# A two-slot ring of weight sums in block 0: ScalarE in place of the load queue issues the stores

## What is computed

```python
h = x + W_out( sig(g_pool) * PoolBranch(n) + sig(g_attn) * W_attn_up(SWA(n)) )    # n = RMSNorm(x)
h = h + W_down( relu(RMSNorm(h) @ W_up)**2 )
y = RMSNorm_final(h)
```

## Time and profile before

| | |
|---|---|
| median of 3 runs | 2518.96 us (2517.32 to 2522.46) |
| the profiled execution | 2517.32 us, span 2515.7 us |
| PE busy | 2372.8 us, 94% of the span |
| DVE, ACT, POOL busy | 1594.0, 1091.8, 345.9 us |
| mean granted TensorE clock | 0.981 of full speed |

### The profile page before, as it was taken

The page is one execution under the profiler, slowest core; times in us unless marked ns, Lnnn a source line. Parts: engine busy times, 40 slices in busy tenths (PEclk is TensorE's granted clock), DMA queues, the critical chain, the costliest instruction groups (busy, mean ns, idle before and its releaser), DMA issues.

```text
span 2515.7 us, 41191 instructions
## 1 busy us (share of the span) xinstructions
PE 2372.8 (94%) x16389; PEld 2192.5 (87%) x16389; DVE 1594.0 (63%) x2432; ACT 1091.8 (43%) x1922; POOL 345.9 (14%) x296
## 2 busy tenths in 40 slices
PE   8999988888788999999999999899999999899997
PEld 8999987878787787999998787899998777799997
DVE  7655733333357556867777656777868655678766
ACT  4533423131343434554553534555554433545543
POOL 1400333333333400000002400000002400000000
PEclk9999999999999999999999999999999999999998
DMA  4223444444455233676674223676665223566774
GB/s 159 73 83 98 151 159 159 160 162 156 166 177 198 66 98 119 230 231 203 203 260 163 73 87 109 218 226 201 219 219 208 95 82 95 190 199 198 231 227 170
DMA packets 149165, 410.37 MB, mean 163 GB/s; under 512 B 17520, under 2 KB 17872, under 8 KB 144880
## 3 DMA queue, kind: packets, MB, share of 16 engines
q1 hardware_dynamic: 144240, 399.00, 48.5%
q10 hardware_dynamic: 4736, 8.75, 0.9%
HBM read 349.65 MB, written 58.13 MB: 162 GB/s over the span
## 4 chain that ended last, share of the span: by engine, by line
PE 66%; DMA 11%; DVE 8%; POOL 6%; ACT 3%; issue 3%; SPq 1%; DVEq 0%; POOLq 0%; ACTq 0%
PE prod L528 30%; DMA weight_split<-wsplit 7%; PE auxB L747 6%; PE auxB L749 6%; PE auxB L748 6%; PE prod L747 5%; PE prod L749 5%; PE prod L748 5%; DMA weight_sums<-wsum 4%; POOL wsum L1644 2%; POOL wsum L1645 2%; POOL wsum L1646 2%; POOL wsum L1643 2%; DVE wring L1183 1%; PE auxB L528 1%
## 5 line engine op out<-in xcount | busy, mean ns | idle before, releaser
L528 PE MATMUL prod<-nH,wm 128*128 128x272 f32 (+1 forms) x3104 | 732.5, 337 | 49.0 <-DVE wm L1183 35.5
L528 PEld LDWEIGHTS prod<-nH,wm 128*128 128x128 f32 x3104 | 507.9, 192 | 112.5 <-issue 39.2
L792 ACT ACTIVATE wm<-raw 128x1024 fp32r<-128x1024 f32 x232 | 234.9, 1012 | 627.0 <-PE prod L528 477.2
L1183 DVE TENSOR_TENSOR wm<-raw,wm 128x1024 fp32r<-128x1024 f32 x232 | 288.1, 1242 | 255.1 <-ACT wm L792 254.1
L528 PE MATMUL prod<-nL,wm 128*128 128x272 f32 (+1 forms) x1552 | 443.4, 335 | 0.0
L792 ACT ACTIVATE wring<-rawq 128x512 fp32r<-128x512 f32 x492 | 307.2, 629 | 285.4 <-PE auxB L749 173.5
L1183 DVE TENSOR_TENSOR wring<-rawq,wring 128x512 fp32r<-128x512 f32 x492 | 334.9, 686 | 102.8 <-PE auxB L749 80.0
L528 PE MATMUL prod<-midH,wm 128*128 128x272 f32 (+1 forms) x1664 | 349.0, 321 | 41.4 <-DVE wm L1183 28.9
L528 PEld LDWEIGHTS prod<-midH,wm 128*128 128x128 f32 x1664 | 263.0, 195 | 64.0 <-issue 24.4
L528 PEld LDWEIGHTS prod<-nL,wm 128*128 128x128 f32 x1552 | 268.0, 192 | 26.7 <-issue 0.5
L747 PE MATMUL auxB<-n7H,wring 128*128 128x256 f32 x768 | 220.5, 287 | 24.6 <-ACT zt L792 14.1
(11 more groups left out here) (173 smaller groups left out, 4477.7 us busy)
## 6 DMA issues: line engine op xcount, KB each, us to landing
raw<-weights SPq DMA_DIRECT2D x200, 512.0 KB, 3.6
wring<-weight_split SPq DMA_DIRECT2D x180, 512.0 KB, 4.1
rawq<-weights SPq DMA_DIRECT2D x288, 256.0 KB, 4.2
rawq<-weight_sums SPq DMA_DIRECT2D x204, 256.0 KB, 4.1
weight_split<-wsplit SPq DMA_DIRECT2D x20, 1536.0 KB, 9.5
weight_sums<-wsum SPq DMA_DIRECT2D x12, 1024.0 KB, 8.0
raw<-weights SPq DMA_DIRECT2D x32, 320.0 KB, 2.8
y<-hT ACTq DMA_DIRECT2D x12, 512.0 KB, 2.8
```

What stands on the lines that cost most here:

```text
L528: ins = nc.tensor.matmul(out[:, s, 0:hi - lo], lhs, rhs[:, lo:hi], start=first, stop=last)
L792: return nc.scalar.activation(out, in_, ACT.Copy, scale=scale)
L1183: return tt(out, x, f(high), ALU.subtract)
```

## The change

ScalarE takes over all stores of the sums. At the end of each odd unit n of block 0's MLP it issues the 1.5 MB store of pair n // 2 (`sums_out`, in split phases, after `s_SL`), then waits for the sums of the **next** pair n // 2 + 1, makes their high part and issues their first store (`sums_high`; in the phases 1, 3, 5 this is the only store, the 1 MB one). Pair 0 is handled before the first unit. DVE's `sums_low` moves from the odd unit of its pair to the even one. SP has no store left between its loads, and its waits for `s_S` and `s_SL` on behalf of the stores go.

```diff
@@ SP
-            def store_sums(p):
-                s, ph = p % 2, p // PAIRS
-                if ph in SPLIT_PHASES:
-                    at = SPLIT_PHASES.index(ph) * PAIRS + p % PAIRS
-                    wait(sp, s_S, p)
-                    sp.dma_start(sums_d[p, :, 3, :], wsum[s][:, 3, :]).then_inc(set_out[s], 16)
-                    wait(sp, s_SL, p)
-                    sp.dma_start(split_d[at], f(wsplit[s][:, :, :, :])).then_inc(set_out[s], 16)
-                else:
-                    wait(sp, s_S, p)
-                    sp.dma_start(sums_d[p], wsum[s][:, :, :]).then_inc(set_out[s], 16)
...
-                if n % 2 and n >= 7:
-                    store_sums((n - 7) // 2)
...
-                    if b == 1 and i in (1, 3, 5):
-                        store_sums(PHASES * PAIRS - 3 + i // 2)
@@ ACT
-            def sums_high(n):
-                p = n // 2
-                if n % 2 == 0 and p // PAIRS in SPLIT_PHASES:
-                    wait(act, s_S, p)
-                    copy(wsplit[p % 2][:, :, 0, :], wsum[p % 2][:, 0:3, :]).then_inc(s_SH.sem, 1)
+            def sums_high(p):
+
+                st, split = p % 2, p // PAIRS in SPLIT_PHASES
+                wait(act, s_S, p)
+                if split:
+                    copy(wsplit[st][:, :, 0, :], wsum[st][:, 0:3, :]).then_inc(s_SH.sem, 1)
+                    act.dma_start(sums_d[p, :, 3, :], wsum[st][:, 3, :]).then_inc(set_out[st], 16)
+                else:
+                    act.dma_start(sums_d[p], wsum[st][:, :, :]).then_inc(set_out[st], 16)
+
+            def sums_out(p):
+                ph = p // PAIRS
+                if ph in SPLIT_PHASES:
+                    wait(act, s_SL, p)
+                    at = SPLIT_PHASES.index(ph) * PAIRS + p % PAIRS
+                    act.dma_start(split_d[at], f(wsplit[p % 2][:, :, :, :])).then_inc(set_out[p % 2], 16)
+
+            def sums_step(n):
+                if n % 2:
+                    sums_out(n // 2)
+                    if n // 2 + 1 < PHASES * PAIRS:
+                        sums_high(n // 2 + 1)
...
-                    sums_high(n)
+                    sums_step(n)
...
                 if b == 0:
                     root("h", 0)
+                    sums_high(0)
@@ DVE
             def sums_low(n):
                 p = n // 2
-                if n % 2 and p // PAIRS in SPLIT_PHASES:
+                if n % 2 == 0 and p // PAIRS in SPLIT_PHASES:
```

## The result

The changed kernel takes **2410.75 us** (median of 4 runs, 2409.84 to 2412.70) against 2519.70 us before (4 runs): a ratio of 0.9568, 95% interval 0.9552 to 0.9585. The direction and the place were right; the forecast gain was about a seventh too small.

What follows compares the result with a forecast made beforehand. The circle of store and sums in block 0's MLP, not PE, was taken as the bound. 98.5 - 8 - 3 + 5.6 = 93 us less than 2517.3 gave 2424, with 1.6 us for the median 2425 us; range 2414 to 2466.

Steps and rivals of the forecast that it cites:

- What bounds the kernel: Block 0's MLP: the circle of store and sums, not PE, sets the pace; 98.5 us lost against 387.2.
- I put 0.5 us on each of these, 8 us, and 3 us on the four turns: Losses left in block 0's MLP: 8 us over 16 split up-projection pairs, 3 us at four turns from up to down.
- The landing: Time for a big store in block 0's MLP to land, taken as 8.5 us.
- POOL on the other hand was taken as 6 us: POOL's time for one pair's sums in block 0's MLP, taken as 6 us.
- inside the limit by 0.6 to 2.3 us: Split up-projection: next sums at E + 4.9 to E + 6.6, limit E + 7.2; E ends product 2p + 1.
- Entry of block 1: PE's wait there for the last of the norm's low parts goes: 5.6 us gained.
- The low end: Whole kernel, no cost at all: 98.5 + 5.6 = 104 us less, 2414 us.
- A (the new wait bites): Split up-projection pairs: sums come 2.4 us late, 38 us lost, 53 us gained in all, 2466 us; chance 0.14.
- B (only the issue time, 22 us): Block 0's MLP: the store still bounds the pair, only SP's issue time goes, 22 us, 2497 us; chance 0.05.
- C (slower): Block 0's MLP: ACT joins the circle; with a landing of 27 us, 37 us slower, 2554 us; chance 0.02.
- D (nothing moves): Block 0's MLP: the loads wait for the same sums, another leg of the circle, 2519 us; chance 0.03.
- What would show it: Signs in block 0's MLP: low-part waits under 12 us, POOL starts 12.1 us apart, last product near 662, landing 7 to 9.5.

Runs made afterwards that it cites:

- The gap experiment: The changed kernel with eleven extra ScalarE copies ahead of the last gained norm tile at the entry of block 1; 2420.89 us.
- the earlier SP place: The kernel before with SP still issuing the stores, but behind the load of unit 2p + 5 instead of 2p + 7; 2416.58 us, ratio 0.9577.
- both halves in place: The kernel before with SP issuing stores behind the load of unit 2p + 5 and parts at the steps of the change; 2413.01 us, ratio 0.9576.
- the steps alone: The kernel before with SP's stores at their old place, but parts made at the steps of the change; 2521.67 us, ratio 0.9997.
- the exchanged order: The changed kernel with ScalarE waiting for and copying the next pair's sums before issuing the big store; 2453.41 us, ratio 0.9733.

## Why the prediction fell short

**What bounds the kernel: right.** The stage at full rate was put at 387.2 us and takes 389.1; the circle of store and sums was the cause. The experiments show it from both sides: opening it on SP alone gives 105 us, closing it again on ScalarE by exchanging two calls takes 43 back.

**The sum's first failed term: "I put 0.5 us on each of these, 8 us, and 3 us on the four turns".** The loss left in the stage is 1.9 us, not 11. Two of its inputs were off, in opposite directions. The landing was taken as 8.5 us "since it now goes beside them" (the loads); it is 5.8 us in the median, 7.7 at most:

```profile
DMA to landing us min/median/max: 5.1/5.8/7.7
```

The stores no longer stand behind the loads: ScalarE issues them by PE's steps, SP issues the loads when sums or splits free a place, and in 17 of the 20 pairs no load was under way when the store went out; the next one followed 0.5 to 4 us later. In the kernel before one event, the arrival of the sums, released both, and two loads stood 0.8 to 1.4 us ahead of nearly every store. POOL on the other hand was taken as 6 us and needs 8.3 in the pair shown above (395.90 to 404.15; the median of all pairs is 6.7). In that pair landing and sums take 6.2 + 8.3 = 14.5 us, exactly what 8.5 + 6 gave: two errors that cancelled, by luck, and with them the forecast of the sums at E + 4.9 to E + 6.6 came near (E + 4.5). What was wrong is the step from there: the arithmetic itself said "inside the limit by 0.6 to 2.3 us", which is no loss, and 8 us were charged on top for fear of the lengthened operations. The other 3 us were for the four turns, where PE now waits 1.6 us in all.

**The second: "Entry of block 1 [...] this goes: 5.6 us".** It is 9.9. The prediction had counted 29 us for the lower granted clock beside 69.4 us of gaps in the stage, and then priced the gap at the entry by its length alone. The gap experiment shows 3 us for 6.0. The stretch also held a second wait, of 0.8 us, that the earlier trace rows does not show. Together the two terms make the miss: 87.5 + 5.6 = 93 forecast, 96.4 + 9.9 and 1.1 for the rest = 107.5 measured.

**The low end failed with it.** "No cost at all would be 98.5 + 5.6 = 104 less" was meant as a bound that nothing could pass, but it held the same short price for the entry. A bound must take each term at its far end; with the clock counted at the rate of the stage (29 us for 69.4 of gaps) the entry would have been 8 us and the end 2412. Even that is 1 to 2 us above the measurement: the bound also needed an allowance for what shifts elsewhere (1.1 us). The stage's own part of the bound, 98.5 us, held (96.4).

**The rivals.** A (the new wait bites) is not what happened, but the longer POOL work shows that it is near: 20 us for two more operations per pair. The prediction's argument against it, that the longest landings had the loads in front, is borne out. B (only the issue time, 22 us) is refuted by the earlier SP place, where the same engine issues the same stores. So the rule beside it, from the Trainium skill's "DMA: Bandwidth & Descriptors", section "Issuing engines are not separate DMA queues", agrees with these runs: with both halves in place, SP and ScalarE as issuers differ by 0.1%. The 105 us come from another thing, the wait that stood ahead of the store. C (slower) needed a landing of 23 us; the longest of a big store in any run is 11.3. D (nothing moves) is what the steps alone give, 2521.67.

**What would show it:** PE's wait for a weight's low part under 12 us (0.2) and the chain on PE came as written. POOL's starts are 12.1 us apart only in the mean (285.9 to 611.3 us over 27 pairs); the single steps run from 6 to 24 us. The last product ended at 653.5 us, not near 662, the landing's median is 5.8 us and not 7 to 9.5, and ScalarE's wait is 14.2 us over six pairs and not 2 to 5 in each, so in most split pairs the sums were there before it asked.

## What to carry to other kernels

Where two buffers give no overlap, look at what stands ahead of the transfer in the program of the engine that issues it: a wait that belongs to the next item turns two places into one. Moving the transfer to another engine helps only if it does not land behind such a wait there as well; try the cheaper edit, an earlier place in the same queue, first. And when a stall of PE is priced, add what the granted clock takes after it, in every place where a stall goes and in the bounds too.

## What the runs showed of the hardware

**The landing of a store depends on what was issued just ahead of it, not on its queue.** The same 1.5 MB takes, in the median, 5.8 us (ScalarE's queue, loads mostly behind it), 6.1 (SP's queue, two loads mostly 0.5 and 1.0 us behind it), 9.5 (SP's queue, 1 MB of loads 0.8 to 1.4 us ahead of it) and 9.5 (ScalarE's queue, one load 0.5 us ahead and one together with it, the run with the store one unit late). In the exchanged order, with one load 0.3 us ahead and one 0.2 us behind, it is 8.9.

**A gap of 6.0 us in PE's work costs about 9**, in the one place measured.

**DVE and POOL stretch each other, and the denser the stage, the more often.** DVE's busy time in the stage goes from 203 to 254 us for the same 204 operations, and POOL's from 157 (117 operations) to 203 (121). By line, in the changed kernel (busy us, mean ns):

```profile
L1185 DVE TENSOR_TENSOR wsplit<-wsum,wsplit 128x1536 fp32r<-128x1536 f32 x20 | 49.2, 2458 | 0.0
L1185 DVE TENSOR_TENSOR midL<-work,midH 128x544 fp32r<-128x544 f32 x32 | 37.1, 1161 | 1.6 <-ACT work L988 1.3
```

The sums' low part takes 2.46 us in the mean instead of 1.81, the hidden tile's 1.16 instead of 0.79. Behind the means stand two lengths each: 1.75 or 2.84 us for the sums, 0.72 or 1.81 us for the hidden tile, in both kernels, the longer one 1.09 us more and only where a POOL operation overlaps. Of the 32 hidden tiles 2 took the longer time before and 13 do now, of the 20 sums 1 and 13. With two more POOL operations per pair DVE's busy time in the stage grows again, to 275 us. The Trainium skill, "SBUF — State Buffer", section "Who interferes with whom", says that a DVE instruction with two SBUF inputs and a GpSimd instruction that reads SBUF share one read port and exclude each other. The operations here are of that kind, and the lengths agree with it; no run here shows that it is the port.
